# Chunk 1's head scaling and splitting moved two slots earlier, and SyncE's weight loads placed ahead of its attention loads

## The chip, the cores and the metric

The kernel runs as one program on one core of a Trainium2 chip. The metric is the device time of one execution in microseconds (us); lower is better. Three runs of the kernel before gave 2776.28, 2778.92 and 2780.08 us, so the median is 2778.92 us.

## The reference, cut to what matters

One layer of a hybrid encoder, for a prompt of 2048 frames of width 1024 and for 64 further frames of a running stream:

```
h    = rmsnorm(x) ; proj = h @ w_in          # a | gate | q | k | v, 5 x 512 columns
c    = silu(layernorm(dwconv31(a * sigmoid(gate)))) @ w_pw
q, k = rmsnorm per head (8 heads of 64) ; v plain
z    = q.k / 8 ; A[t,s] = sigmoid(z[t,s]) * prod_{s<j<t} sigmoid(-z[t,j])   for s < t
o    = A @ v
x    = x + concat(c, o) @ w_out
x    = x + relu(rmsnorm(x) @ w_ff1)^2 @ w_ff2
```

Everything is float32. k, v and the last 30 values of a * sigmoid(gate) are outputs as well as x.

## The kernel before, in words

Each product is made of three matmuls over a high and a low part (`mm3`, lines L2020 to L2022; `project`, L2088 to L2090): an operand is split into `hi`, the float32 value rounded by a copy, and `lo`, the rest. The prompt is worked in four chunks of 512 frames. The order of the work on every engine is written out in Python: each engine has its own block, and the engines meet only at semaphores. A wait therefore holds everything that stands behind it on its engine. TensorE is the block `pe`, VectorE `dve`, ScalarE `act`, GpSimd `pool`, and SyncE (`sp`) issues every DMA.

The change lies in `front()`, a stage of 92 slots (`FRONT`, numbered t = 0 to 91) in which chunk 0's convolution and attention run beside chunk 1's input projection. Each engine walks over the same slots.

TensorE does the gated columns in slots 0 to 31, four slots for each slab. From slot 32 (`KVQ_AT`) it does twelve projection events of four slots each: events 0 to 3 are k for the four 128-frame tiles, 4 to 7 are v, and 8 to 11 are q. The result of event s is taken over from slot `event_out(s)` = 36 + 4s on. I call this slot E in the list of what is done with an event of k or q:

- E: ScalarE squares the result (L1307), and VectorE sums the squares per head, multiplies the result with the gain and makes the mean (`kq_sums`, L1703, L1708, L1713). The multiplication frees the PSUM bank.
- E+2: GpSimd raises the mean to the power -1/2 (`kq_rstd`, L1137). In its slot this stands behind the attention products of the slot.
- E+4: VectorE scales the heads (`kq_norm`, L1745), which waits for that power.
- E+5: ScalarE copies the high part (`kvq_high`, L1325), and SyncE stores k (`store_kv`, L847).
- E+6: VectorE makes the low part (`kvq_low`, L1722).
- E+8 and E+10: TensorE transposes the two halves (`turn_packed`, L2100). The second waits for ScalarE's copy of the first (L1338, at E+9 and E+11). At E+12 SyncE stores the transposed heads. The q events 9 to 11 (`OUT_TURN`) are transposed later, in `out(0)`.

A v event is copied at E (L1303), split at E+1 and E+2 (L1319, L1727) and stored at E+5.

Chunk 0's attention runs in slots 31 to 57 (`att_steps`), 41 steps in 27 slots, so one or two in a slot. A piece z is 128 queries of one head against 128, 256, 384 or 512 keys, in turn. At step z TensorE makes its scores (L2221) and ScalarE its two sigmoids (L1451, L1452). At step z+1 VectorE scans (L1859) and GpSimd multiplies (L1174). At z+3 TensorE transposes (L2231) and ScalarE copies (L1463), at z+4 VectorE makes the low part (L1869), and at z+5 comes the product with the values (L2254). Two pieces make a pair. A finished pair is put into one of two buffers `ohl` (ScalarE L1475, VectorE L1881) and stored by SyncE at z+8 (L959). ScalarE waits for the store of the pair before the last before it writes `ohl` again. SyncE loads the queries of pair n+3 (`load_queries`, L895) when pair n's scores are done, and the keys and values of head n+2 (L886, L891) when head n is done.

The weights pass through a ring of eight slabs (`RING`) of 1 MB. `weights(t)` (L774 for a slab already split) issues all the loads whose time has come by a table of ticks, strictly in their order, each behind a wait for the slab that leaves its place. Between slots 31 and 57 it issues loads in two slots only: four slabs for v in slot 32, which take the places of two slabs of the pointwise projection (used in slots 22 to 28) and of the last two gated slabs (used up in slots 27 and 31), and four slabs for q in slot 48, which take the places of the k slabs (used up in slot 47).

VectorE also does chunk 1's convolution taps (`convolve`, L1651), three in two slots from slot 58 on, and the low parts of new weight slabs (L1611), four of them in slot 71. Behind slot 79 TensorE goes on to `out(0)` (L2388 to L2390), which waits for VectorE's multiplication of event 11.

Of the kernel before, what the change touches and what calls it, by code (L numbers as in the profile page):

```python
# [37 lines left out]
def tiles(c):  # L38

    t = [(P * i, P) for i in range(CHUNK // P)]  # L40
    return t + [(CHUNK, DEC)] if c == NC - 1 else t
# [50 lines left out]
def att_steps_total(c):  # L92
    return sum(len(seq) + TAIL for seq in passes(c))
# [41 lines left out]
def ln0(c):  # L135

    return (LATE[c] + 1) // 2
# [18 lines left out]
def att_first(c):  # L156
    return pw_slot(c) + pw_step(c) * CB + 1


def att_past(c):  # L160

    return 58 if c == 0 else 116
# [6 lines left out]
def att_steps(c, slot):  # L169

    a, b, n = att_first(c), att_past(c), att_steps_total(c)
    if slot < a or slot >= b:
        return range(0)
    return range(n * (slot - a) // (b - a), n * (slot - a + 1) // (b - a))
# [7 lines left out]
def event_out(s):  # L182

    return KVQ_AT + 4 * (s + 1)
# [75 lines left out]
TICK = ticks()  # L260
# [32 lines left out]
def load_tick(n):  # L293
    return use_of(n - RING)[1] if n >= RING else -8.0 + 1.5 * n
# [17 lines left out]
def build(nc, x_prompt, x_sample, cache_k, cache_v, state_conv, g_mix, w_in, w_dw, b_dw, g_cn, b_cn, w_pw,  # L312
# [3 lines left out]
    with ctx:  # L316
# [422 lines left out]
        def _(sp):  # L739
# [36 lines left out]
            def store_slab(n):  # L776
                kind, c, j = W[n]
                sp.wait_ge(lo_done, FIRST[n] + 1)
                sp.dma_start(w_d[W_ID[kind, j]], w_s[:, n % RING, :].bitcast(F32)).then_inc(w_st[n % RING], 16)

            def weights(t):

                while True:
                    n, i = at["load"], at["store"]
                    if i < len(FIRST_ORDER):
                        m = FIRST_ORDER[i]
                        if m < n and (load_tick(m) + STORE_LAG <= t or (n < len(W) and m == n - RING and load_tick(n) <= t)):
                            store_slab(m)
                            at["store"] += 1
                            continue  # L790
                    if n < len(W) and load_tick(n) <= t:
                        load_slab(n)
                        at["load"] += 1
                        continue
                    return
# [113 lines left out]
            def att_begin(c):  # L909

                nt = len(tiles(c))
                for m in (2 * nt - 2, 2 * nt - 1):
                    sp.wait_ge(kq_st[m % 2], kq_stores(c, m))
                for i in (nt - 2, nt - 1):
                    sp.wait_ge(*value_stored(c, i))
                sp.wait_ge(cache_out, 32)
                sp.wait_ge(kvq_ps, 12 * c + 3 * nt)
                for s in range(c, -1, -1):
                    load_keys(c, 0, s)
                    load_values(c, 0, s)  # L920
                if c == 0:
                    load_keys(0, 1, 0)
                    load_values(0, 1, 0)
                pairs = [q for q in ATT[c, 0] if q.t == 0 and q.diag]
                for q in pairs[:3]:
                    if q.hp >= 3:
                        sp.wait_ge(z_ps, att_end(c - 1, "z"))
                    load_queries(c, q)
# [59 lines left out]
            def front():  # L988
                for t in range(FRONT):
                    for late in tail_turn(0, t, 2):  # L990
                        store_turned(0, late)
                    for s in range(len(kvq_events(1))):
                        if t == event_out(s) + 5:
                            store_kv(1, s)
                        if t == event_out(s) + 12 and s not in OUT_TURN:
                            store_turned(1, s)
                    if t == ln0(0):
                        att_begin(0)
                    for step in att_steps(0, t):
                        att(0, step)  # L1000
                    weights(TICK["win", -1, t])
                    m = pw_part(0, t - 1)
                    if m is not None:
                        store_pw(0, m)
                    if t >= att_past(0) + 2 and t in MIX_AT:
                        load_mix_part(0, *divmod(MIX_AT.index(t), 2))
                    if t == MIX_AT[-1] + 3:
                        load_norm(0)
                    if t == event_out(len(kvq_events(1)) - 1):
                        for k in range(2):  # L1010
                            sp.wait_ge(vo_out[k], 16 * 4)
                        for k in (2, 3):
                            sp.wait_ge(*value_stored(1, k))
                        for i in range(2):
                            load_resid(0, i)
                for i in range(2):
                    sp.wait_ge(kq_st[i], kq_stores(1, 2 + i))
                for i in range(2, 4):
                    load_resid(0, i)
# [204 lines left out]
        def _(act):  # L1224
# [134 lines left out]
            def front():  # L1359
                evs = kvq_events(1)  # L1360
                for t in range(FRONT):
                    splits_until(TICK["win", -1, t] + 2)
                    for late in tail_turn(0, t, 1):
                        kvq_turned(0, late, TURNED)
                    for piece, step in ln_step(0, t):
                        ln(0, piece, step)
                    m = pw_part(0, t - 1)
                    if m is not None:
                        pw(0, m)
                    if t == att_first(0) - 1:  # L1370
                        for ev in range(2):
                            act.wait_ge(pw_st[ev], 32)
                    steps = att_steps(0, t)
                    for step in steps[:1]:
                        att_sigmoids(0, step)
                    for m in range(CB):
                        if t == gated_out(m):
                            gate(1, 2 * m + 1, 0, front_bank("ag", 2 * m + 1))
                    for s, (sec, i, m) in enumerate(evs):
                        if t == event_out(s):  # L1380
                            kvq_out(1, s, front_bank("event", s))
                        if t == event_out(s) + (1 if sec == "v" else 5):
                            kvq_high(1, s)
                        for q in range(2):
                            if t == event_out(s) + 9 + 2 * q and sec != "v" and s not in OUT_TURN:
                                kvq_turned(1, s, [front_bank("turn", s)] * 2, (q,))
                    for step in steps[:1]:
                        att_later(0, step)
                    for step in steps[1:]:
                        att_sigmoids(0, step)  # L1390
                        att_later(0, step)
# [212 lines left out]
        def _(dve):  # L1604
# [160 lines left out]
            def front():  # L1765
                evs = kvq_events(1)
                done = 0
                for t in range(FRONT):
                    splits_until(TICK["win", -1, t] + 2)
                    if t < ln0(0):  # L1770
                        convolve(0, late_taps(0, t))
                    if t == ln0(0):
                        history(1)
                        dve.wait_ge(consts, 6)
                    for piece, step in ln_step(0, t):
                        ln(0, piece, step)
                    m = pw_part(0, t - 1)
                    if m is not None:
                        pw(0, m)
                    for step in att_steps(0, t):  # L1780
                        att_parts(0, step)
                        att_mask(0, step)
                    for m in range(CB):
                        if t == gated_out(m):
                            gated(1, m, 0, front_bank("ag", 2 * m))
                            dve.wait_ge(ag_u, 4 + m + 1)
                    for s, (sec, i, m) in enumerate(evs):
                        if t == event_out(s):
                            kq_sums(1, s, front_bank("event", s))
                        if t == event_out(s) + 4:  # L1790
                            kq_norm(1, s)
                        if t == event_out(s) + (2 if sec == "v" else 6):
                            kvq_low(1, s)
                    convolve(1, range(done, second_upto[t]))
                    done = second_upto[t]
# [653 lines left out]
```

## Time and profile before

| what | value |
| --- | --- |
| runs, us | 2776.28, 2778.92, 2780.08 |
| span of the profiled execution (its own time, first to last instruction), us | 2777.2 |
| TensorE busy | 2687.2 us (97%) |
| VectorE busy | 1663.9 us (60%) |
| ScalarE busy | 1069.5 us (39%) |
| GpSimd busy | 453.3 us (16%) |
| mean granted clock of TensorE | 0.990 |

A share of busy time is a mean over the whole program. The change touches some 140 us, from 225 us to 370 us of the span, in which the engines stand differently. There the page alone doesn't say what decides, and the rows of the trace are needed.

### The profile page before, as it was taken

The page shows a single profiled execution, that of the slowest core. Times are in us where ns is not written, and L with a number is a line of the kernel's source. Part 1 is how long each engine was busy: PE and PEld are TensorE (multiplying, and loading weights), DVE is VectorE, ACT ScalarE, POOL GpSimd, SP SyncE. Part 2 cuts the span into 40 slices and gives each one's busy share as a digit, 9 for nine tenths or more (in the row PEclk, how much of TensorE's full clock was granted, in tenths as well). Part 3 has the DMA queues.
Part 4 walks back from the last instruction along what each step waited for, and adds up shares of the span by engine and source line. Part 5 has one row for each costly group of instructions (what it writes and reads, how often), then busy time and mean ns, then how long its engine had stood idle before and what let it go on. Part 6 is the DMA issues. An engine that isn't in the chain of part 4 may idle for free. (4 is left out here: it accounts for less than half of the span.)

```text
span 2777.2 us, 37645 instructions
## 1 busy us (share of the span) xinstructions
PE 2687.2 (97%) x14000; PEld 2270.3 (82%) x14000; DVE 1663.9 (60%) x2621; ACT 1069.5 (39%) x2146; POOL 453.3 (16%) x462
## 2 busy tenths in 40 slices
PE   8988899999999999999999999999999999999999
PEld 6757778788887887788888797778888887998998
DVE  6996767577763576377775368627888842222122
ACT  4434524455552122355553212335666631221211
POOL 2122210022210010032221102103333310000000
PEclk9999999999999999999999999999999999999999
DMA  9795797697769568455554747845355456443532
GB/s 330 255 349 188 237 355 266 259 336 253 256 218 375 214 233 282 184 209 185 168 187 165 284 186 237 291 163 190 118 181 191 150 188 248 187 177 122 212 152 95
DMA packets 262048, 616.21 MB, mean 222 GB/s; under 512 B 23217, under 2 KB 159409, under 8 KB 213741
## 3 DMA queue, kind: packets, MB, share of 16 engines
q1 hardware_dynamic: 261869, 613.80, 61.8%
q8 instruction: 115, 1.88, 0.3%
q14 instruction: 64, 0.52, 0.1%
HBM read 444.79 MB, written 168.94 MB: 221 GB/s over the span
## 5 line engine op out<-in xcount | busy, mean ns | idle before, releaser
L2020 PE MATMUL ps<-h2T_hi,w_s 128*128 128x512 f32 (+2 forms) x1312 | 469.2, 358 | 7.9 <-DMA w_s<-w_scratch 3.9
L2022 PE MATMUL ps<-h2T_hi,w_s 128*128 128x512 f32 (+2 forms) x1312 | 458.3, 349 | 0.0
L1174 POOL TENSOR_TENSOR beta<-beta,stay 128x512 f32<-128x512 f32 (+3 forms) x328 | 313.0, 955 | 889.5 <-DVE stay L1859 853.4
L2021 PE MATMUL ps<-h2T_lo,w_s 128*128 128x512 f32 (+2 forms) x1312 | 457.9, 349 | 0.0
L1929 DVE TENSOR_TENSOR resid<-ps,resid 128x512 f32<-128x512 f32 x256 | 174.6, 687 | 261.3 <-PE ps L2285 260.6
L1451 ACT ACTIVATE stay<-ps 128x512 f32<-128x512 f32 (+3 forms) x328 | 174.8, 533 | 347.2 <-PE ps L2221 227.1
L2283 PE MATMUL ps<-w_s,hid_hi 128*128 128x512 f32 x768 | 308.3, 401 | 0.0
L2284 PE MATMUL ps<-w_s,hid_lo 128*128 128x512 f32 x768 | 299.9, 390 | 0.0
L2285 PE MATMUL ps<-w_s,hid_hi 128*128 128x512 f32 x768 | 299.8, 390 | 0.0
L1526 ACT ACTIVATE ps<-ps 128x512 f32<-128x512 f32 (+1 forms) x160 | 81.3, 508 | 542.7 <-PE ps L2022 542.7
L2020 PEld LDWEIGHTS ps<-h2T_hi,w_s 128*128 128x128 f32 x1312 | 248.0, 189 | 38.3 <-DMA w_s<-w_scratch 4.0
L1859 DVE TENSOR_TENSOR_SCAN stay<-stay,stay,ones 128x512 f32<-128x512 f32 x192 | 274.4, 1430 | 0.0
L2022 PEld LDWEIGHTS ps<-h2T_hi,w_s 128*128 128x128 f32 x1312 | 247.8, 189 | 30.9
L2021 PEld LDWEIGHTS ps<-h2T_lo,w_s 128*128 128x128 f32 x1312 | 248.2, 189 | 26.6 <-issue 1.0
L1651 DVE SCALAR_TENSOR_TENSOR cacc<-uT,vecs,cacc 128x512 f32<-128x512 f32 (+1 forms) x360 | 259.6, 777 | 1.5
L1939 DVE TENSOR_TENSOR hid_lo<-ps,hid_hi 128x512 fp32r<-128x512 f32 x96 | 66.3, 691 | 261.8 <-ACT hid_hi L1536 261.8
L1869 DVE TENSOR_TENSOR aT_lo<-ps,aT_hi 128x512 fp32r<-128x512 f32 (+3 forms) x328 | 189.6, 578 | 14.6 <-ACT aT_hi L1463 8.8
L2221 PE MATMUL ps<-a_k,a_q 128*128 128x512 f32 (+3 forms) x640 | 186.9, 371 | 8.8 <-DMA a_k<-k_scratch 6.9
L2231 PE MATMUL ps<-ident,beta 128*128 128x128 f32 (+1 forms) x1104 | 175.1, 274 | 7.4 <-DVE aT_lo L1869 7.3
L1463 ACT CAST aT_hi<-ps 128x512 fp32r<-128x512 f32 (+3 forms) x328 | 173.6, 529 | 19.3 <-PE ps L2231 14.7
L1452 ACT ACTIVATE beta<-ps 128x512 f32<-128x512 f32 (+3 forms) x328 | 173.6, 529 | 0.0
L2285 PEld LDWEIGHTS ps<-w_s,hid_hi 128*128 128x128 f32 x768 | 144.2, 188 | 31.9
(217 smaller groups left out, 5179.1 us busy)
## 6 DMA issues: line engine op xcount, KB each, us to landing
w_s<-w_scratch SPq DMA_DIRECT2D x282, 1024.0 KB, 7.5
w_scratch<-w_s SPq DMA_DIRECT2D x94, 1024.0 KB, 8.3
w_raw<-in_w_ff SPq DMA_DIRECT2D x64, 512.0 KB, 5.7
a_k<-k_scratch SPq DMA_DIRECT2D x80, 256.0 KB, 3.8
a_v<-v_scratch SPq DMA_DIRECT2D x80, 256.0 KB, 4.0
a_q<-q_scratch SPq DMA_DIRECT2D x64, 256.0 KB, 4.4
w_raw<-in_w_in SPq DMA_DIRECT2D x20, 512.0 KB, 7.7
mix_scratch<-ohl SPq DMA_DIRECT2D x66, 128.0 KB, 3.0
```

What stands on the lines that cost most here:

```text
L1174: nc.gpsimd.tensor_tensor(v[0:q.r, 0:n], v[0:q.r, 0:n], stay_of(q.z)[0:q.r, 1:n + 1], ALU.mult).then_inc(s_a, 1)
L1651: nc.vector.scalar_tensor_tensor(out=acc, in0=uT[:, k, tap:tap + wd], scalar=vecs[:, k, tap:tap + 1], in1=acc, op0=ALU.mult, op1=ALU.add). ...
L1859: nc.vector.tensor_tensor_scan(v[0:q.r, 0:q.n][:, ::-1], v[0:q.r, 0:q.n][:, ::-1], ones[0:q.r, 0:1].to_broadcast([q.r, q.n]), init, ALU.mu ...
L1869: ins = nc.vector.tensor_tensor(aT_lo[:, o, 0:full, q.t * P:q.t * P + q.r], bank[:, 0:full * q.r].rearrange("p (a b) -> p a b", a=full), a ...
L2020: nc.tensor.matmul(out, w[0], x[0], start=start, stop=False)
L2021: nc.tensor.matmul(out, w[0], x[1], start=False, stop=False)
L2022: return nc.tensor.matmul(out, w[1], x[0], start=False, stop=stop)
L2221: ins = nc.tensor.matmul(ps[0:q.r, Z_BANK + q.z % 2, 0:q.n], x, a_k[:, k0:k0 + q.n], start=v == 0, stop=v == 1)
L2231: ins = nc.tensor.transpose(ps[0:w, T_BANK + q.z % 2, b * q.r:(b + 1) * q.r], beta[q.z % 4][0:q.r, b * P:b * P + w], ident[0:q.r, 0:q.r])
L2283: nc.tensor.matmul(o, hid_hi[x][:, k, q0:q0 + r], wh[:, c0:c0 + BANK], start=k == 0, stop=False)
L2284: nc.tensor.matmul(o, hid_lo[x][:, k, q0:q0 + r], wh[:, c0:c0 + BANK], start=False, stop=False)
L2285: ins = nc.tensor.matmul(o, hid_hi[x][:, k, q0:q0 + r], wl[:, c0:c0 + BANK], start=False, stop=k == 3)
```

## The change

Chunk 1's heads are scaled by VectorE at E+2 instead of E+4, their high part is copied by ScalarE at E+3 instead of E+5, and their low part is made at E+4 instead of E+6. SyncE's store of k and v comes at E+3 instead of E+5. GpSimd's power stays at E+2 and the transposes stay where they were. On SyncE `weights` stands ahead of the attention's loads and stores in each slot.

```diff
@@ SyncE, front()
-                        if t == event_out(s) + 5:
+                        if t == event_out(s) + 3:
                             store_kv(1, s)
...
                     if t == ln0(0):
                         att_begin(0)
+                    weights(TICK["win", -1, t])
                     for step in att_steps(0, t):
                         att(0, step)
-                    weights(TICK["win", -1, t])
@@ ScalarE, front()
-                        if t == event_out(s) + (1 if sec == "v" else 5):
+                        if t == event_out(s) + (1 if sec == "v" else 3):
                             kvq_high(1, s)
@@ VectorE, front()
-                        if t == event_out(s) + 4:
+                        if t == event_out(s) + 2:
                             kq_norm(1, s)
-                        if t == event_out(s) + (2 if sec == "v" else 6):
+                        if t == event_out(s) + (2 if sec == "v" else 4):
                             kvq_low(1, s)
```

## Rows read from the trace of the kernel before

**Rows 1.** The page's first line: the span.

```profile
span 2777.2 us, 37645 instructions
```

**Rows 2.** Waits of TensorE, 130 to 420 us: total us, times, longest us.

```profile
PE ps L2100 <- ACT kqT_second L1338: 9.9, 3, 5.8
PE ps L2100 <- DVE packed L1722: 9.1, 2, 4.7
```

**Rows 3.** Stretches: length, busy PE, PEld, DVE, ACT, POOL, granted clock, DMA share, GB/s.

```profile
246.00:250.00 4.00, 3.06 (x14) 3.10 (x15) 0.85 (x2) 0.93 (x4) 0.41 (x1) 0.50 0.30 106
250.00:254.00 4.00, 4.00 (x14) 3.37 (x14) 0.80 (x2) 1.06 (x4) 0.00 (x0) 0.55 0.36 98
...
257.00:302.50 45.50, 40.07 (x251) 34.41 (x249) 43.60 (x76) 31.76 (x86) 22.08 (x23) 1.00 0.67 194
```

**Rows 4.** SyncE's issues in order of time: start, length.

```profile
214.31 11.41 SPq L967 DMA_DIRECT2D mix_scratch<-pwo  x3
...
230.86 2.46 SPq L774 DMA_DIRECT2D w_s<-w_scratch  x4
233.36 0.74 SPq L886 DMA_DIRECT2D a_k<-k_scratch  x1
...
291.11 1.14 SPq L959 DMA_DIRECT2D mix_scratch<-ohl  x1
...
292.96 2.03 SPq L774 DMA_DIRECT2D w_s<-w_scratch  x4
...
296.67 0.75 SPq L959 DMA_DIRECT2D mix_scratch<-ohl  x1
```

**Rows 5.** DMAs issued from 226 to 234 us: KB each, median us to landing.

```profile
a_q<-q_scratch SPq DMA_DIRECT2D x1, 256.0 KB, 3.1
a_k<-k_scratch SPq DMA_DIRECT2D x1, 256.0 KB, 12.3
```

**Rows 6.** TensorE's scores of pieces 6 and 8, in order of time.

```profile
237.27 0.34 PE L2221 MATMUL ps<-a_k,a_q 128*128 128x384 f32 x1
...
246.94 0.45 PE L2221 MATMUL ps<-a_k,a_q 128*128 128x128 f32 x1 [6.07 <-DMA a_k<-k_scratch]
```

**Rows 7.** GpSimd's power of k events 0 and 1, in order of time.

```profile
258.10 1.64 POOL L1137 TENSOR_TENSOR hrs<-hrs,neghalf 128x8 f32<-128x8 f32 x1
...
272.18 3.43 POOL L1137 TENSOR_TENSOR hrs<-hrs,neghalf 128x8 f32<-128x8 f32 x1
```

**Rows 8.** VectorE's next instruction behind its attention work of slots 38 and 42.

```profile
258.22 1.23 DVE L1859 TENSOR_TENSOR_SCAN stay<-stay,ones 128x512 f32<-128x512 f32 x1
...
272.24 0.67 DVE L1722 TENSOR_TENSOR packed<-kn,packed 128x512 fp32r<-128x512 f32 x1
```

**Rows 9.** ScalarE's copies of two pairs into `ohl`, in order of time.

```profile
299.36 0.40 ACT L1475 CAST ohl<-osb 64x256 fp32r<-64x256 f32 x1
...
309.61 0.40 ACT L1475 CAST ohl<-osb 64x256 fp32r<-64x256 f32 x1 [7.22 <-DMA mix_scratch<-ohl]
```

**Rows 10.** VectorE in the q events, in order of time.

```profile
346.21 4.62 DVE L1611 TENSOR_TENSOR w_s<-w_raw,w_s 128x1024 fp32r<-128x1024 f32 x4
...
353.94 2.08 DVE L1651 SCALAR_TENSOR_TENSOR cacc_second<-uT,vecs,cacc_second 128x512 f32<-128x512 f32 x3
355.93 0.69 DVE L1722 TENSOR_TENSOR packed<-kn,packed 128x512 fp32r<-128x512 f32 x1
...
366.81 0.69 DVE L1703 TENSOR_REDUCE hss<-sqr_second 128x8 f32<-128x512 f32 x1 [1.16 <-ACT sqr_second L1307]
367.41 0.68 DVE L1708 TENSOR_TENSOR raw_kq<-ps,gq 128x512 f32<-128x512 f32 x1
```

**Rows 11.** GpSimd's power of q event 8.

```profile
343.73 2.07 POOL L1137 TENSOR_TENSOR hrs<-hrs,neghalf 128x8 f32<-128x8 f32 x1 [26.99 <-DVE hrs L1713]
```

**Rows 12.** TensorE's two waits around the q events, in order of time.

```profile
356.76 1.09 PE L2100 MATMUL ps<-ident,packed 128*128 128x128 f32 x4 [4.39 <-DVE packed L1722]
...
368.46 0.47 PE L2388 MATMUL ps<-w_s,mix_first_hi 128*128 128x512 f32 x1 [2.31 <-DVE raw_kq L1708]
```

## The prediction

> **What bounds the kernel now.** The profiled execution spans 2777.2 us [rows 1]; the median of the runs shown, 2778.92, stands 1.7 above it, and I add my sum to the median. Over the whole span TensorE is the bound. I read the waits of TensorE next, cut to the stretch that the change touches. There the reader is to see TensorE's transposes waiting 9.9 us for ScalarE's copies and 9.1 us for VectorE's low parts [rows 2]. Then the stretches: from 257.0 to 302.5 us VectorE is busy 43.60 of 45.50 us and TensorE 40.07 [rows 3]. So in chunk 0's attention VectorE is the bound, and TensorE's and ScalarE's waits there are its shadow. The order of time of each engine shows the rest.
>
> **The first slab train, slot 32.** Before, SyncE goes through the attention of slot 32 first: it waits for the scores of piece 1 and loads queries, the slabs follow at 230.86, and head 2's keys at 233.36 [rows 4]. The queries in front of the slabs landed in 3.1 us, the keys behind them in 12.3 [rows 5], at about 246.5, and piece 8 stood 6.07 us for them [rows 6]. After it TensorE runs at half of its full clock, 0.50 and 0.55 in the next two stretches of 4 us [rows 3], that is mostly at 1.2 instead of 2.4 GHz: 3.06 x 0.50 + 4.00 x 0.45 = 3.3 us lost. The whole thing costs 6.07 + 3.3 = 9.4 us.
>
> After the change SyncE reaches the slabs when its last store of the pointwise projection is out, at 214.31 + 11.41 = 225.7 [rows 4]. The first three slabs wait for places that were free by then; the fourth needs the end of slot 31, about 229.9. So the train starts 5 us sooner. But the queries of pair 3, which piece 6 needs at 237.27 [rows 6], now stand behind all four slabs. Before, a train begun at 230.9 let the keys behind it land at 246.5, 15.6 us on; one begun at 225.8 lets the queries land at about 241.3. Piece 6 then waits 4.0 us. From piece 6 to piece 8 there are 240.87 - 237.27 = 3.6 us of work (240.87 is 246.94 less its wait [rows 6]), so piece 8 comes at 244.9 instead of 246.9, its keys being there by 243. That is 2.0 us won, and the clock costs again between nothing (5.3 us won) and the same 3.3 (2.0 won). I take the middle, **-3.5 us**; the ends are -0.5 (queries another 1.5 us late) and -9.4 (queries in time).
>
> **Scaling at E+2 in the k events, slots 38, 42, 46 and 50.** GpSimd's power stands in the very slot to which the scaling moves, behind the attention products of that slot. So a wait is added: VectorE reaches the scaling right behind its last scan of the slot, and GpSimd still has the product of that scan and the power before it. Event 0: VectorE is free at 258.22 [rows 8], the power ends at 258.10 + 1.64 = 259.74 [rows 7]: 1.6 us, but VectorE still had idle time just before, so I take 1.0. Event 1: VectorE is free at 272.24 [rows 8]; the power starts at 272.18 and took 3.43 [rows 7] beside a busy VectorE. With VectorE waiting I take the shortest power, 1.64: 1.6 us; the upper end is 3.4. Event 2 is of the same kind, 1.8 with its own power of about 2. Behind the waiting scaling stand the next scans; ScalarE's sigmoids, GpSimd's products and so TensorE's transposes wait for these. With VectorE idle only 1.9 of 45.5 us [rows 3] nothing covers the wait: 1.0 + 1.6 + 1.8 = **+4.4 us**, ends 0 and 9.0 (3.4 + 3.4 + 2.2). The scaling itself, ScalarE's high part and the low part are only moved: same instructions, same durations, no price. Nor is anything won: of the two waits for a low part, 9.1 us in all [rows 2], one is the 4.39 of rows 12 in the q events and the other, 4.7, lies ahead of `front()`, so none is in the k events.
>
> What the row shows is a power of 8 elements stretched from 1.64 to 3.43 us [rows 7]. The Trainium skill ("SBUF — State Buffer", the section on the two sides of the memory) says that GpSimd and a VectorE instruction with two SBUF inputs lock each other out of a shared port pair for whole instructions. By that rule an idle VectorE leaves the power at its shortest and the sum is 4.4; by the stretched row it would be 9.0. No row shows a power beside an idle VectorE in this stage.
>
> **The second slab train, slot 48, and event 3.** Before, the slabs go out at 292.96, behind the store of a pair (291.11) and a load of queries; the next pair's store at 296.67 lies behind them [rows 4] and held ScalarE 7.22 us, until 309.61 [rows 9]. Now the slabs go when slot 47 is done, about 290.5, 2.5 us sooner, and the store of 291.11 and the queries stand behind them. By the same 15.6 us they land at 306.1. The copy at 299.36 [rows 9] needs that store, so ScalarE stops one pair sooner, from 299.4 to 306.1. The next copy comes after its own work of 309.61 - 7.22 - 299.36 = 3.0 us, at 309.0 or a little later, its store landed. That is 0.6 won. But event 3's scaling stands in slot 50, whose work before ran under ScalarE's stall and now comes behind it. Its wait, 1.4 us (event 0's 1.6 less what a shorter product takes), is no longer covered: -0.6 + 1.4 = **+0.8 us**; ends -2.5 (the full lead of the train) and +2.5 (the queries of the last pair land late too).
>
> **The q events.** Here TensorE waits 4.39 us for VectorE's low part of event 8 [rows 12], the wait that an earlier E+4 removes. VectorE's new order from 343.6 on: three taps of 0.66 (2.08 for three with the last one's tail [rows 10]) to 345.6; the power ends at 343.73 + 2.07 = 345.8 [rows 11]; scaling 0.6 to 346.5, one tap 347.1, four slabs 4.5 (4.62 with the tail [rows 10]) to 351.7, two taps to 353.0, low part to 353.6. That is 2.9 us sooner than 355.93 + 0.6, and TensorE starts sooner by this. Then on to event 11: sums 1.3 (354.9), three taps (356.9), power until 357.1, scaling (357.8), three taps (359.8), low part (360.4), sums (361.7), three taps (363.7), power until 363.9, scaling (364.6), three taps (366.6), low part of event 10 (367.2), reduction of event 11 (367.8), and its multiplication, which `out(0)` needs, begins at 367.8 instead of 367.41 [rows 10]. So TensorE wins 2.9 us at slot 76, and gives them and 0.4 more back at `out(0)`: VectorE was idle only 1.16 us before event 11 [rows 10] and now does one low part more ahead of it. TensorE then stands some 5 us there instead of 2.31 [rows 12]. An idle time of 6 us was followed by half clock above, and this one may be: I add 0.6. **+1.0 us**, ends -1.2 (no waits for powers, the idle time used up) and +2.5.
>
> SyncE's stores at E+3 wait for the scaling one slot before, as they did at E+5, and nothing urgent is behind them. In slots 64 and 80 `weights` has no attention beside it; the order changes nothing there. In `out(0)` VectorE and ScalarE are some 1 to 4 us later with the low part of event 11 and the first sum, which TensorE asks for only with its sixth of eight groups: no price.
>
> **Sum.** -3.5 + 4.4 + 0.8 + 1.0 = +2.7 us: 2778.9 + 2.7 = 2781.6. What a measurement can tell from no change is 0.2%, 5.6 us, that is 2773.4 to 2784.5. I forecast **no change that can be told**.
>
> **Rivals.**
> A. Slower: GpSimd's power keeps its stretched length while VectorE waits (place: slots 38, 42, 46). The waits are 9.0 instead of 4.4: +7.3, 2786.2. For it: 3.43 in the one row; against it: 1.64 in the other [rows 7]. From 7.3 us of waits on, the sum is over 5.6.
> B. Faster: the queries land before piece 6 and the second train gives its full 2.5, and the scaling's waits fall into gaps that ScalarE leaves VectorE, 2.0 in all: -9.4 - 2.5 + 2.0 + 1.0 = -8.9, 2770.0. For it: VectorE idles when TensorE is slow, 0.80 of 4.00 us busy [rows 3]; against it: 43.60 of 45.50, and 12.3 us behind slabs [rows 5].
> C. The slabs don't start sooner, because all four wait for slot 31: the train starts at 229.9, the queries land at 245.5, piece 8 comes at 249.1: +2.2 instead of -3.5, sum +8.4, 2787.3. For it: the fourth slab does wait for it; against it: the three others' places are free long before.
> D. All of it is hidden behind other waits: 2778.9. For it: each of the four terms trades one wait for another.
>
> **Chances.** Forecast 0.45, A 0.15, B 0.17, C 0.10, D 0.10, and 0.03 for slower by other sizes of these terms. Faster by over 0.2% is B, 0.17; slower is A, C and the rest, 0.28; within it 0.55. The forecast's own range is 2777 to 2784.5. For 8 in 10 the range reaches into B, A and C: 2773 to 2788.
>
> **What the profile after would show.** Right: slabs issued from about 226, scores of piece 6 waiting some 4 us for `a_q`, none for `a_k`; VectorE waiting 1.4 to 1.8 us for GpSimd at L1745, four times in the k events; ScalarE's stop moved from the copy at 309.6 to the one before; TensorE's wait at L2100 in slot 76 down to about 1.5, and the one at L2388 up to 5. Wrong: no wait of VectorE at L1745, or an `out(0)` that starts over 2 us sooner relative to slot 58, or slabs still issued at 230. If VectorE waits little and piece 6 waits not at all, my forecast is too high.

## The result, and the profile after

The changed kernel takes 2782.91 us (median of 8 runs, 2779.98 to 2787.21) against 2775.81 us for the kernel before (8 runs, 2774.36 to 2780.08): ratio 1.0025, 95% interval 1.0015 to 1.0035, that is 4 to 10 us slower. The forecast was 2781.6 us, +2.7. The time lies in the range, and the direction holds; the step of +2.7 us was two fifths of the measured one. That the two times, 2781.6 and 2782.91, are only 1.3 us apart is in part luck: the forecast's base of 2778.92 stood 3.1 us above this comparison's median of the kernel before, and its step was 4.4 us too small. Its words were "no change that can be told", with 5.6 us as the limit; 7.1 us, with an interval clear of zero, is past that limit, on the slower side. Two single executions of the experiments below, 7991 us of scale_only and 5405 us of slabs_only, were in a slow state and do not enter the ratios.

The page's first lines after (before: [rows 1]). TensorE's busy time is 3.5 us longer for the same 14000 matmuls, the rest of the 5.0 us between the spans is idle time:

```profile
span 2782.2 us, 37645 instructions
...
PE 2690.7 (97%) x14000; PEld 2271.7 (82%) x14000; DVE 1663.7 (60%) x2621; ACT 1068.8 (38%) x2146; POOL 449.7 (16%) x462
```

SyncE's issues after (start, length; before: [rows 4]). The first train leaves at 225.12 with three slabs, the fourth waits for the end of slot 31; the queries for piece 6 (229.54) and the keys (231.92) stand behind all four. In slot 48 two stores of pairs (297.65 and 298.99) stand behind the second train; it starts 1.2 us later than the 292.96 of [rows 4], in a kernel that is some 4 us behind by then:

```profile
225.12 4.37 SPq L774 DMA_DIRECT2D w_s<-w_scratch  x4
229.54 0.68 SPq L895 DMA_DIRECT2D a_q<-q_scratch  x1
231.92 0.32 SPq L886 DMA_DIRECT2D a_k<-k_scratch  x1
...
294.16 2.93 SPq L774 DMA_DIRECT2D w_s<-w_scratch  x4
297.13 0.47 SPq L891 DMA_DIRECT2D a_v<-v_scratch  x1
297.65 0.62 SPq L959 DMA_DIRECT2D mix_scratch<-ohl  x1
298.32 0.63 SPq L895 DMA_DIRECT2D a_q<-q_scratch  x1
298.99 0.63 SPq L959 DMA_DIRECT2D mix_scratch<-ohl  x1
```

The landing of these queries (issued from 226 to 231 us: KB, median us to landing; before 3.1, [rows 5]):

```profile
a_q<-q_scratch SPq DMA_DIRECT2D x1, 256.0 KB, 11.7
```

TensorE's scores of pieces 6 and 8 (before: [rows 6]). The wait has gone from the keys of piece 8 to the queries of piece 6, and piece 8 waits for nothing:

```profile
241.32 0.44 PE L2221 MATMUL ps<-a_k,a_q 128*128 128x384 f32 x1 [4.59 <-DMA a_q<-q_scratch]
...
246.36 0.30 PE L2221 MATMUL ps<-a_k,a_q 128*128 128x128 f32 x1
```

GpSimd's power and VectorE's scaling of the four k events, each in order of time (before: [rows 7, 8]). VectorE waits each time, and each power has its shortest length:

```profile
256.10 1.64 POOL L1137 TENSOR_TENSOR hrs<-hrs,neghalf 128x8 f32<-128x8 f32 x1
272.12 1.64 POOL L1137 TENSOR_TENSOR hrs<-hrs,neghalf 128x8 f32<-128x8 f32 x1
289.19 1.63 POOL L1137 TENSOR_TENSOR hrs<-hrs,neghalf 128x8 f32<-128x8 f32 x1
312.29 1.64 POOL L1137 TENSOR_TENSOR hrs<-hrs,neghalf 128x8 f32<-128x8 f32 x1
```

```profile
257.78 0.69 DVE L1745 TENSOR_TENSOR kn<-raw_kq,hrs 128x512 f32<-128x512 f32 x1 [1.60 <-POOL hrs L1137]
...
273.79 0.69 DVE L1745 TENSOR_TENSOR kn<-raw_kq,hrs 128x512 f32<-128x512 f32 x1 [1.55 <-POOL hrs L1137]
290.85 0.69 DVE L1745 TENSOR_TENSOR kn<-raw_kq,hrs 128x512 f32<-128x512 f32 x1 [1.73 <-POOL hrs L1137]
...
313.96 0.69 DVE L1745 TENSOR_TENSOR kn<-raw_kq,hrs 128x512 f32<-128x512 f32 x1 [1.41 <-POOL hrs L1137]
```

ScalarE's stop for the store of a pair (before, with 7.22 us: [rows 9]). It comes one pair sooner, as forecast, and lasts 7.86 us where 6.7 (299.4 to 306.1) was forecast; the next copy, at 313.07, waits for no store:

```profile
310.47 0.40 ACT L1475 CAST ohl<-osb 64x256 fp32r<-64x256 f32 x1 [7.86 <-DMA mix_scratch<-ohl]
```

In the q events, TensorE's waits (before: [rows 12]), and behind them VectorE's low part of event 10 and the multiplication of event 11 (before: [rows 10]):

```profile
358.97 0.63 PE L2100 MATMUL ps<-ident,packed 128*128 128x128 f32 x4 [1.42 <-DVE packed L1722]
...
364.65 0.66 PE L2100 MATMUL ps<-ident,packed 128*128 128x128 f32 x4 [1.52 <-ACT kqT_late L1338]
373.85 0.77 PE L2388 MATMUL ps<-w_s,mix_first_hi 128*128 128x512 f32 x1 [5.81 <-DVE raw_kq L1708]
```

```profile
371.61 0.69 DVE L1722 TENSOR_TENSOR packed<-kn,packed 128x512 fp32r<-128x512 f32 x1
372.21 0.68 DVE L1703 TENSOR_REDUCE hss<-sqr_second 128x8 f32<-128x512 f32 x1
372.81 0.68 DVE L1708 TENSOR_TENSOR raw_kq<-ps,gq 128x512 f32<-128x512 f32 x1
```

A slot has one projection matmul that opens it on TensorE, so the starts of these in two traces, both taken from slot 32, show slot by slot where time goes. This table is worked out so from the profiled executions (us behind the kernel before; minus is ahead; "out" is the first matmul of the output product, L2388). The names are those of the experiments below:

```
slot   after scale_only slabs_only power_early k_only q_only train32 train48 two_early q_spread both_spread spread_scaled
 37    -2.9   -1.7       -1.9       -3.3       -1.3   -1.1   -6.2    -1.1     -8.0      -7.9     -9.3        -9.3
 39    -1.8   -1.7       -0.9       -2.5       -1.3   -1.2   -5.2    -1.1     -8.0      -7.9     -8.3        -8.5
 42     0.7    0.2       -0.3       -1.6        0.9   -1.2   -4.6    -1.2     -7.7      -7.8     -7.7        -7.5
 46     2.7    2.3       -0.3       -0.9        2.6   -1.2   -4.6    -1.1     -7.7      -7.7     -7.7        -6.9
 49     4.4    3.9       -0.3       -1.0        4.3   -1.2   -4.6    -1.2     -7.7      -7.7     -7.7        -7.0
 52     6.0    3.5       -0.7       -1.4        3.7   -0.7   -4.8    -0.8     -7.4     -13.8    -13.8       -14.1
 75     5.9    3.3       -0.3       -1.3        3.7   -0.1   -4.9    -0.2     -7.5     -13.1    -13.1       -14.2
 76     3.3    0.7       -0.2       -3.9        3.7   -2.7   -4.9    -0.4     -7.5     -13.1    -13.1       -16.8
out     6.1    3.5       -1.5       -1.1        2.5    0.1   -6.1    -1.4     -8.7     -13.3    -14.4       -14.0
```

After is ahead by 2.9 us in slot 37 and goes back by 2.5, 2.0 and 1.7 us where the scalings of events 0, 1 and 2 stand, by another 1.6 at event 3, and by 0.2 over the q events.

All columns are taken against one trace of the kernel before, and that trace is a slow one in slot 32. scale_only, k_only, q_only and train48 have its order of loads there, and yet they are 1.1 to 1.7 us ahead in slot 37; q_only and train48 are still 1.2 ahead in slot 42. The difference lies in the clock behind the wait of piece 8. In the trace of before it was 0.50 and 0.55 in two stretches of 4 us [rows 3]; in train48 it came back in the second of them:

```profile
245.00:249.00 4.00, 2.99 (x14) 3.02 (x15) 0.85 (x2) 0.85 (x4) 0.41 (x1) 0.50 0.32 114
249.00:253.00 4.00, 4.00 (x19) 3.37 (x19) 1.69 (x4) 1.66 (x5) 0.43 (x1) 0.88 0.42 109
```

So a column that differs from zero by less than some 1.5 us says nothing by itself; columns are to be compared with each other.

### The profile page after: what moved, and what is told of

It reads as the page before. It is cut to its first block and busy times, and to the rows that moved or that the text cites. A ratio compares the mean times of both kernels' runs of the same rounds, so it can differ in the third digit from the quotient of the medians.

```text
span 2782.2 us, 37645 instructions
## 1 busy us (share of the span) xinstructions
PE 2690.7 (97%) x14000; PEld 2271.7 (82%) x14000; DVE 1663.7 (60%) x2621; ACT 1068.8 (38%) x2146; POOL 449.7 (16%) x462
## 5 line engine op out<-in xcount | busy, mean ns | idle before, releaser
L2231 PEld LDWEIGHTS ps<-ident,beta 128*128 128x128 f32 (+1 forms) x1104 | 134.4, 141 | 45.6 <-issue 19.1
```

The costliest lines, as they stand in the source:

```text
L2231: ins = nc.tensor.transpose(ps[0:w, T_BANK + q.z % 2, b * q.r:(b + 1) * q.r], beta[q.z % 4][0:q.r, b * P:b * P + w], ident[0:q.r, 0:q.r])
```

## The experiments

Ratios are to the kernel before on the same chip, with 95% intervals; 0.001 is 2.8 us.

**scale_only**: the scaling's part of the change alone, SyncE's order as before.

```diff
+                    for step in att_steps(0, t):
+                        att(0, step)
                     weights(TICK["win", -1, t])
-                    for step in att_steps(0, t):
-                        att(0, step)
```

> Only the scaling, the high and low parts and the stores of k and v are moved two slots earlier; SyncE's order is that of before. Theory: VectorE's waits for GpSimd's power in slots 38, 42 and 46 (1.6 us each, seen in the changed kernel) are on the path, so this alone costs 4 to 8 us against before, and piece 8 stands about 6 us for its keys as before. Rival 1 (the slab order does the damage, the scaling is free): within 1 us of before. Rival 2 (both halves cost the same): about +3.5 us.

Measured: 2782.99 us, ratio 1.0019 (1.0010 to 1.0028), 3 to 8 us slower. Piece 8 still waits 5.7 us for its keys. The table shows three losses of 1.9, 2.1 and 1.6 us between slots 39 and 49 and none at event 3: there the wait lies under ScalarE's stop, as this row shows beside the 7.22 of [rows 9]; it is shorter by 0.6:

```profile
313.68 0.40 ACT L1475 CAST ohl<-osb 64x256 fp32r<-64x256 f32 x1 [6.60 <-DMA mix_scratch<-ohl]
```

Rival 1, a free scaling, is out. Rival 2, +3.5 us for each half, lies inside this interval; the next run takes it out.

**slabs_only**: SyncE's part alone, on the kernel before.

```diff
+                    weights(TICK["win", -1, t])
                     for step in att_steps(0, t):
                         att(0, step)
-                    weights(TICK["win", -1, t])
```

> Only SyncE's order is changed: weight slabs ahead of the attention in each slot; the scaling stays at E+4. Theory: the first train wins 2 to 4 us by slot 38 (piece 6 waits 4.6 us for queries, piece 8 not at all), the second costs or wins under 1.5 us, so 1 to 4 us faster than before. Rival 1 (queries and stores behind the slabs cost): 3 to 7 us slower than before. Rival 2 (both trains are hidden later): within 1 us.

Measured: 2776.78 us, ratio 0.9998 (0.9988 to 1.0008). The interval is 3 us faster to 2 us slower: rival 1's loss is out, the theory's 1 to 4 us is not, and the middle is rival 2's number. But nothing was hidden later. The win is small where it is made: against q_only and train48, which have the old order in slot 32, slabs_only is 0.8 us ahead in slot 37 and 0.9 behind in slot 42.

**train32** and **train48**: the new order in slot 32 alone, or in slot 48 alone.

```diff
+                    if t == 32:      # train48: t == 48
+                        weights(TICK["win", -1, t])
                     for step in att_steps(0, t):
                         att(0, step)
                     weights(TICK["win", -1, t])
```

> The kernel before, with the weight slabs ahead of the attention in slot 32 alone. Theory: piece 6 waits 4.5 to 5 us for its queries, piece 8 for nothing, and relative to slot 32 TensorE is 1 to 3 us ahead by slot 38 and under 1 us from slot 40 on; 0 to 1 us faster than before. Rival (the train's lead of 5 us is kept): 3 to 5 us faster.

> The kernel before, with the weight slabs ahead of the attention in slot 48 alone. Theory: ScalarE stops one pair sooner and some 0.5 us less long; relative to slot 47 TensorE is within 1 us of before at slot 53. Rival 1 (the 2.5 us of the earlier train are won): 2 to 3 us ahead. Rival 2 (the queries of the last pair, behind the slabs, come late): 1 to 3 us behind.

Measured: train32 2777.19 us, 0.9998 (0.9990 to 1.0007); train48 2777.02 us, 0.9996 (0.9988 to 1.0005). Neither can be told from before, and the rival of train32 (3 to 5 us faster) is out. In train48 ScalarE stops one pair sooner, but not for a shorter time, as was expected:

```profile
304.90 0.40 ACT L1477 CAST ohl<-osb 64x256 fp32r<-64x256 f32 x1 [7.74 <-DMA mix_scratch<-ohl]
```

train48 goes from 1.2 ahead to 0.2 ahead between slot 49 and slot 75. That loss of 1.0 is not the train's: q_only, with the old order in slot 48, goes from 1.2 to 0.1 ahead there, and slabs_only, with the new one, loses nothing. So the train alone costs nothing that can be seen, and nothing of its lead of 2.5 us is kept.

The profiled execution of train32 was 5.6 us ahead in slot 38 and 4.6 in slot 42, where 1 to 3 and under 1 had been expected; slabs_only has the same order in slot 32 and was 0.3 ahead in slot 42. The rows of piece 6 in the two, slabs_only first:

```profile
243.86 0.69 PE L2221 MATMUL ps<-a_k,a_q 128*128 128x384 f32 x1 [4.89 <-DMA a_q<-q_scratch]
```

```profile
241.37 0.44 PE L2223 MATMUL ps<-a_k,a_q 128*128 128x384 f32 x1 [2.85 <-DMA a_q<-q_scratch]
```

and the stretch from 244 to 248 us behind them, in the same order (columns as in [rows 3]; the granted clock is the third number from the end):

```profile
244.00:248.00 4.00, 4.00 (x15) 3.63 (x16) 1.96 (x3) 1.81 (x4) 0.86 (x1) 0.50 0.02 9
```

```profile
244.00:248.00 4.00, 4.00 (x28) 3.58 (x26) 2.90 (x5) 2.68 (x8) 1.63 (x2) 1.00 0.38 86
```

The length of the wait alone does not decide whether the clock falls. power_early, described below, has the same order in slot 32 and waited shortest of the three, and its clock fell all the same:

```profile
238.78 0.69 PE L2221 MATMUL ps<-a_k,a_q 128*128 128x384 f32 x1 [2.76 <-DMA a_q<-q_scratch]
```

```profile
240.00:244.00 4.00, 4.00 (x15) 3.49 (x14) 1.96 (x3) 1.81 (x4) 0.86 (x1) 0.50 0.04 13
```

Against q_only and train48 in slot 42, the term of this train is +0.9 us in slabs_only, -0.4 in power_early and -3.4 in train32. From the first to the second the wait is 2.1 us shorter. From the second to the third it is the same within 0.1, and the 3.0 us between them go with the clock: it falls to its lower level of 1.2 GHz (15 matmuls in 4 us) or not (28). What decides that is left open by these runs. The medians say that a small win, or none, is the usual case.

**power_early**: the changed kernel, with GpSimd's power taken one slot forward. It does not take the wait away but makes it end sooner.

```diff
-                        if t == event_out(s) + 2:
+                        if t == event_out(s) + 1:
                             kq_rstd(1, s)
```

> The changed kernel with GpSimd's power moved from slot E+2 to slot E+1, so that it is finished when VectorE comes to the scaling at E+2; nothing else differs. Theory: the three waits of 1.6 us and the one of 1.4 us at the scaling go in the k events, and the time falls by 4 to 8 us against the changed kernel, to before's or up to 3 us below it. Rival (the waits only stand in for idle time that VectorE would have had, and the moved instructions themselves delay its scans): within 1.5 us of the changed kernel, some 7 us slower than before.

Measured: 2778.55 us, ratio 1.0001 (0.9992 to 1.0009), 6.7 us below the changed kernel's ratio. VectorE's waits at the scaling, from 225 to 380 us (total us, times, longest), in the changed kernel and in this one; the four that are left are those of the q events:

```profile
DVE kn L1745 <- POOL hrs L1137: 7.1, 8, 1.7
```

```profile
DVE kn L1745 <- POOL hrs L1137: 0.8, 4, 0.2
```

The rival, that the moved instructions cost and not their wait, is out: VectorE has the same instructions in the same order, and the loss is gone.

**k_only** and **q_only**: the scaling, the parts and the stores moved for the k events alone (s < 4), or for the q events alone (s >= 8), on the kernel before.

```diff
-                        if t == event_out(s) + 4:
+                        if t == event_out(s) + (2 if s < 4 else 4):     # q_only: s >= 8
                             kq_norm(1, s)
```

and the same condition at the high part, the low part and the store.

> The kernel before with scaling, parts and stores two slots earlier for the k events alone (0 to 3). Theory: VectorE waits 1.6, 1.6, 1.7 and 1.4 us for GpSimd's power, each of the first three puts TensorE 1.7 to 2.5 us back, the fourth lies under ScalarE's stop as with the scaling moved for all events: 3 to 6 us slower than before. Rival (the loss of that run came from the q events): within 1.5 us of before.

> The kernel before with scaling, parts and stores two slots earlier for the q events alone (8 to 11); k and v events and SyncE's order as before. Theory: TensorE's wait in slot 76 falls from 4.4 us to 1.5 and the one at the start of the output product rises from 2.3 to 5.8, so the output product starts 0 to 1.5 us later: within 2 us of before. Rival (the shorter wait in slot 76 is kept): 2 to 3 us faster.

Measured: k_only 2781.33 us, ratio 1.0015 (1.0006 to 1.0023); q_only 2778.44 us, 1.0004 (0.9995 to 1.0013). In the table k_only loses 2.2, 1.7 and 1.7 us at events 0 to 2. Its rival, that scale_only's loss came from the q events, is out. TensorE in q_only:

```profile
352.63 0.63 PE L2100 MATMUL ps<-ident,packed 128*128 128x128 f32 x4 [1.43 <-DVE packed L1722]
353.73 0.50 PE L2088 MATMUL ps<-w_s,hT_second_hi 128*128 128x512 f32 x1 [0.47 <-DVE raw_kq L1708]
358.30 0.66 PE L2100 MATMUL ps<-ident,packed 128*128 128x128 f32 x4 [1.54 <-ACT kqT_late L1338]
367.51 0.77 PE L2388 MATMUL ps<-w_s,mix_first_hi 128*128 128x512 f32 x1 [5.79 <-DVE raw_kq L1708]
```

The wait of 4.39 us has become 1.43, TensorE is 2.6 us further ahead in slot 76 than in slot 75, and all of it goes into the wait of 5.79 for VectorE's event 11. The output product starts 0.2 us later than slot 75 would have it. By its ninth matmul of L2388 q_only has lost another 1.0 us (the changed kernel 0.5, scale_only 0.5) against the trace of before: all three begin the output product at a granted clock of 0.50, which in before was 0.65 over its first 4 us.

**two_early**: the kernel before, but only two slabs of the v train go ahead of slot 32's attention; `weights` takes a bound.

```diff
+                    weights(TICK["win", -1, t], W_AT["v", 1, 2])   # slabs below this number only
                     for step in att_steps(0, t):
                         att(0, step)
                     weights(TICK["win", -1, t])
```

> The kernel before, but in each slot SyncE issues slabs up to the second of the v train ahead of the attention and the others behind it as before: two slabs leave at about 226 us, then the queries of pair 3, then the other two slabs. The scaling and the second train are those of before. Theory (the stall is a matter of what stands in front of a load in the DMA queue): the queries stand behind 2 MB instead of 4 and land before piece 6 needs them, the keys of head 2 land some 4 to 5 us sooner than before, so piece 8 waits 2 us or less and TensorE keeps its clock: 5 to 9 us faster than before. Rival (the attention after piece 8 is bound by VectorE and eats what is won there): 0 to 3 us faster.

Measured: 2768.51 us, ratio 0.9967 (0.9955 to 0.9979), 6 to 12 us faster than before. The scores of pieces 6 and 8 (a line is one number later here):

```profile
237.38 0.34 PE L2222 MATMUL ps<-a_k,a_q 128*128 128x384 f32 x1
...
242.07 0.30 PE L2222 MATMUL ps<-a_k,a_q 128*128 128x128 f32 x1 [1.09 <-DMA a_k<-k_scratch]
```

Piece 6 waits no more, piece 8 waits 1.09 us, and the lead of 8.0 us made by slot 37 stays 7.7 through the stretch in which VectorE is the bound. The same two early slabs, without the other two in front of the queries, make the whole difference to train32 (0.9998).

**q_spread** and **both_spread**: two_early, with the slabs for q one at a time behind the attention of slots 48, 50, 52 and 54; both_spread also puts the third and fourth slab for v behind slots 33 and 35. **spread_scaled** is both_spread with the scaling moved as in the change and the power at E+1.

```diff
-                    weights(TICK["win", -1, t])
+                    weights(TICK["win", -1, t], W_AT["v", 1, 2] if t == 32 else W_AT["v", 1, 3] if 33 <= t < 35 else
+                            W_AT["q", 1, 0] + (t - 46) // 2 if 48 <= t < 56 else len(W))
```

> Two slabs of the v train ahead of slot 32's attention as in the last run of this kind, and now the four slabs for q one at a time, behind the attention of slots 48, 50, 52 and 54; they are used from slot 64 on. Theory: a pair's store then stands behind one slab and not four, ScalarE's stop of 6.4 us for it falls under 1 us, TensorE keeps its clock there: 5 to 9 us faster than the version with two early slabs, 13 to 18 us faster than before. Rival (VectorE, busy 96% there, is the bound and the stop only lets it catch up): under 3 us faster than the version with two early slabs.

> As the run with the q slabs one at a time, and the third and fourth slab for v behind the attention of slots 33 and 35 instead of both in slot 32, so that the keys of piece 8 stand behind one slab less. Theory: TensorE's last wait for a load in this stage, 1.1 us at piece 8, goes: 0 to 1.5 us faster than with the q slabs spread alone. Rival (the next loads, queries and keys of head 3, now stand behind the fourth slab and piece 10 waits): 1 to 3 us slower than it.

> Both trains spread, and the scaling moved as in the change, with GpSimd's power one slot earlier so that nothing waits for it. Theory: with the DMA waits gone the attention is bound by VectorE, whose work the moved scaling neither shortens nor lengthens, and the q events give back in the output product what they win: within 1.5 us of both trains spread without the scaling moved. Rival (the earlier low parts now free TensorE and ScalarE in the k events): 2 to 4 us faster.

Measured: q_spread 2763.11 us, 0.9952 (0.9939 to 0.9964); both_spread 2763.26 us, 0.9943 (0.9931 to 0.9956); spread_scaled 2766.03 us, 0.9951 (0.9938 to 0.9965). ScalarE's stop for a pair's store was still there in two_early:

```profile
302.39 0.40 ACT L1476 CAST ohl<-osb 64x256 fp32r<-64x256 f32 x1 [6.38 <-DMA mix_scratch<-ohl]
```

and the copies of q_spread from 289 to 300 us have none:

```profile
289.02 0.40 ACT L1476 CAST ohl<-osb 64x256 fp32r<-64x256 f32 x1
293.52 0.40 ACT L1476 CAST ohl<-osb 64x256 fp32r<-64x256 f32 x1
299.71 0.41 ACT L1476 CAST ohl<-osb 64x256 fp32r<-64x256 f32 x1
```

The table gives 6.1 us for it between slots 49 and 52; by the ratios q_spread is 4.2 us faster than two_early, with overlapping intervals, so that the rival's "under 3 us" is not excluded by the times. That the stop costs is read from the rows and the table. both_spread and q_spread can't be told apart. Both beat the kernel before and the changed one; both_spread is 12 to 19 us faster than before. The scaling moved without its wait adds nothing: in the profile of spread_scaled 2.6 us are won in slot 76 and 2.8 given back before "out", and the time is the same within the interval.

## Why the prediction was right, and where its sizes were off

**VectorE as the bound of the attention, and the added wait: right in place, too small in price.** The waits were put at 1.6, 1.6 and 1.8 us and measured 1.60, 1.55 and 1.73, event 3's at 1.4 and measured 1.41. The term was 4.4 us on the path, because I let idle time cover 0.6 of event 0's. Nothing was covered: slots 39 to 49 cost 5.6 us in scale_only and 5.6 in k_only, that is 1.6 to 2.2 for each wait of 1.6 to 1.7. The changed kernel loses 6.2 there, but slabs_only and train32 lose 0.6 of it without any wait at the scaling. This term is the one mis-sized most surely, by some 1.2 us: 0.6 are the cover that I supposed, and why a wait costs up to 0.6 more than its length these runs leave open. Rival A, the stretched power, is out: the power took 1.63 or 1.64 us in all four waits, against 3.43 in [rows 7]. By the rule on the shared port pair cited in the prediction (the Trainium skill, "SBUF — State Buffer") this is what an idle VectorE should give, and the trace agrees. It does not show that the rule is the reason for the 3.43: event 0's power in [rows 7] took the same 1.64 beside a scan that began 0.12 us behind it [rows 8].

**The first train: right in mechanism, over-sized.** The queries of piece 6 landed at about 241.3, as worked out, and piece 6 waited 4.59 us where 4.0 was forecast; piece 8 waited for nothing. -3.5 us was forecast. slabs_only and train32 measure 0.9998 each, so the term is +2 to -3 us by their intervals and about -0.6 by their middle. The middle that I took supposed a clock that stays up half of the time; it fell in the changed kernel, in slabs_only and in power_early, and stayed up in train32. Besides, the price of the old order, 3.3 us for the clock, was read from a trace in which the clock stayed low longer than in train48. This is the second mis-sized term. Rivals B and C are out as wholes: B's landing before piece 6 didn't come about, C's late start neither (225.12).

**The second train with event 3: +0.8 forecast.** It was put together of -0.6 for the train and +1.4 for event 3's wait. The train alone shows no loss and no win (slabs_only stands the same in slots 49 and 75; train48's 1.0 is q_only's too), and the changed kernel shows +1.6 with the wait. The 2.5 us of lead were not won. That event 3's wait is covered while the train stands in its old place, and uncovered in the new one, fits scale_only (no loss) and the changed kernel (1.6), and so do their rows: the two halves of the change cost more together than alone. It rests on one profile of each, in a stretch in which traces without that wait differ by over 1 us among themselves. Their ratios alone add up to 1.0017, against 1.0025 (1.0015 to 1.0035) together; that surplus is within the intervals, and only the profiles show it.

**The q events: +1.0 forecast, +0.7 to +1.2 in the profiles.** VectorE's new order was worked out row by row and came as written: TensorE's wait 1.42 instead of 4.39 us, the other one 5.81 instead of 2.31. The start of `out(0)` lost 0.2 where 0.4 was forecast. The 0.6 for a lower clock showed as 0.5 in the changed kernel and in scale_only and 1.0 in q_only. By q_only's ratio the term is -1.4 to +3.6 us. This term came out right.

**The sum.** With the measured sizes, -0.6 + 5.6 + 1.6 + 0.7 = +7.3 against 7.1 between the medians. The sizes come partly from ratios and partly from single profiles, so that they meet this closely is no proof of each. Rival D, all hidden, is out.

## What to carry to other kernels

A consumer that is moved nearer to its producer on another engine must be checked against what stands in front of the producer in its own queue; move the producer first (here one slot forward for GpSimd's power took 6.7 us of loss away). A prefetch that is not due for many slots must not stand as a block in front of small loads and stores that are due soon: two slabs ahead of them and the other six one at a time gave 12 to 19 us here, while only exchanging which of the small ones stand behind the block gave nothing that can be told. And a wait that is removed ahead of an engine with a backlog comes back at the next meeting with that engine. Last, two executions of the same code differed by over 1 us in one stage here: with a term of that size, look whether another trace with the same code in that stage shows it too.

## What the runs showed of the hardware that was not expected

A power of 8 elements per partition on GpSimd took 1.63 to 1.64 us in the k events of the changed kernel, with VectorE waiting for it. Beside a busy VectorE, in the kernel before, it took 1.64, 3.43, 2.08 and 1.64 us in the k events and 2.07 in the q events, so that a busy VectorE stretched it only in some places. A 256 KB load took 3.1 us from issue to landing ahead of four slabs of 1 MB and 11.7 us behind them on the same queue; the Trainium skill ("DMA: Bandwidth & Descriptors", Queues, rings and completion order) says that each DMA engine takes its descriptors in ring order, and the trace agrees. TensorE's granted clock fell to 0.50, 1.2 GHz, at idle times of 2.76, 4.89 and 6.07 us for a DMA, and stayed at 1.00 behind one of 2.85 us in the same place as the first two: of two waits of nearly the same length one cost the clock and the other did not.
